# A mixture-of-experts stage with 33 static blocks of 64 rows and five weight slots

## The reference

```python
def hier_moe(xn, w_rg, b_rg, w_re, b_re, w_gate, w_up, w_down):
    t = xn.reshape(-1, D_MODEL)
    ...   # top-1 of 4 groups, then top-2 of its 8 experts: combine (576, 32), two entries a row
    def step(acc, xs):
        wg, wu, wd, c = xs                      # (1024, 256), (1024, 256), (256, 1024) float32
        hdn = jax.nn.silu(t @ wg) * (t @ wu)
        return acc + c[:, None] * (hdn @ wd).astype(jnp.float32), None
```

## Time and profile before

| | us |
|---|---|
| three runs of the kernel | 1416.87, 1423.91, 1422.7 |
| their median | 1422.7 |
| profiled execution: its own time as the page gives it, the span | 1420.8 |
| expert stage in it, first gate-and-up matmul to last copied result | 1003.6 to 1386.1 |
| after it, gather and final norm | 1386.1 to 1420.8 |

### The profile page before, as it was taken

How to read it: one execution, slowest core, us unless ns; L and a number is a source line. 1 busy time by engine, 2 the same in 40 slices (tenths; PEclk the granted TensorE clock), 3 DMA queues, 4 the chain that set the end, 5 groups by cost and what they waited for, 6 DMA issues and landing times.

```text
span 1420.8 us, 22301 instructions
## 1 busy us (share of the span) xinstructions
PE 1264.7 (89%) x8549; PEld 1130.7 (80%) x8549; DVE 796.2 (56%) x938; ACT 616.8 (43%) x819; POOL 67.5 (5%) x132
## 2 busy tenths in 40 slices
PE   5989999999999999999989989982788888888880
PEld 4989999999999999999989989982455555555550
DVE  4437374473755736547365444326567677677645
ACT  5434243343433434335343222232566666666632
POOL 0001010010100101001010000003000000000002
PEclk9999999999999999999999999965799999999995
DMA  5261121211121112121102235533888888888836
GB/s 186 95 208 54 58 71 61 72 47 61 65 67 56 61 61 65 53 71 61 63 22 80 80 103 164 211 136 127 293 319 322 321 323 325 316 329 328 313 126 220
DMA packets 49434, 212.80 MB, mean 150 GB/s; under 512 B 5920, under 2 KB 8496, under 8 KB 37104
## 3 DMA queue, kind: packets, MB, share of 16 engines
q1 hardware_dynamic: 41200, 194.05, 39.2%
q0 software_dynamic: 2928, 10.05, 2.1%
q10 hardware_dynamic: 5264, 8.13, 1.6%
HBM read 181.25 MB, written 30.96 MB: 149 GB/s over the span
## 4 chain that ended last, share of the span: by engine, by line
PE 78%; DVE 7%; ACT 6%; DMA 4%; issue 3%; POOL 1%; SPq 0%; ACTq 0%; DVEq 0%; POOLq 0%
PE proj L620 25%; PE proj L1337 15%; PE wideB L1358 6%; PE proj L987 5%; PE wideA L378 4%; PE proj L930 3%; PE wideB L370 3%; PE wideB L384 2%; PE wideA L1324 2%; DVE xbl L1426 2%; ACT xbh L1422 2%; PE small L987 2%; DMA wraw<-in_w_in 1%; PE small L1178 1%; POOL scr_rows L1783 1%
## 5 line engine op out<-in xcount | busy, mean ns | idle before, releaser
L620 PE MATMUL proj<-xnh,whi 128*128 128x288 f32 x1152 | 347.9, 302 | 11.1 <-DVE xnl L1868 6.3
L620 PE MATMUL proj<-xnl,whi 128*128 128x288 f32 x1152 | 347.2, 301 | 0.0
L620 PE MATMUL proj<-xnh,wlo 128*128 128x288 f32 x1152 | 347.0, 301 | 0.0
L620 PEld LDWEIGHTS proj<-xnh,whi 128*128 128x128 f32 x1152 | 217.9, 189 | 12.3 <-issue 5.7
L1414 DVE TENSOR_TENSOR elo<-eraw,ehi 128x4096 fp32r<-128x4096 f32 x64 | 214.6, 3354 | 19.8 <-ACT ehi L1404 19.8
L620 PEld LDWEIGHTS proj<-xnl,whi 128*128 128x128 f32 x1152 | 217.8, 189 | 0.0
L620 PEld LDWEIGHTS proj<-xnh,wlo 128*128 128x128 f32 x1152 | 217.8, 189 | 0.0
L1337 PE MATMUL proj<-ehi,xbh 128*80 128x512 f32 x256 | 111.0, 433 | 33.9 <-DVE xbl L1426 33.9
L632 DVE TENSOR_TENSOR wlo<-wraw,whi 128x1024 fp32r<-128x1024 f32 x72 | 95.1, 1321 | 58.1 <-ACT whi L628 57.1
L1404 ACT ACTIVATE ehi<-eraw 128x4096 fp32r<-128x4096 f32 x32 | 116.1, 3627 | 0.5
L1337 PE MATMUL proj<-elo,xbh 128*80 128x512 f32 x256 | 109.9, 429 | 0.0
(11 more groups left out here) (329 smaller groups left out, 2370.2 us busy)
## 6 DMA issues: line engine op xcount, KB each, us to landing
wraw<-in_w_in SPq DMA_DIRECT2D x72, 512.0 KB, 3.3
eraw<-in_w_gate SPq DMA_DIRECT2D x32, 1024.0 KB, 4.9
eraw<-in_w_up SPq DMA_DIRECT2D x32, 1024.0 KB, 7.2
eraw<-in_w_down SPq DMA_DIRECT2D x32, 1024.0 KB, 5.5
wraw<-in_w_out SPq DMA_DIRECT2D x24, 512.0 KB, 3.7
xb<-scr_rows SPq DMA_DIRECT2D x32, 320.0 KB, 6.0
scr_y<-yout SPq DMA_DIRECT2D x32, 320.0 KB, 5.7
scr_gate<-gate ACTq DMA_DIRECT2D x16, 288.0 KB, 2.1
```

The costliest lines, as they stand in the source:

```text
L620: mm = pe.matmul(out, w[:, kc, :], x[:, kc, hh * HALF:(hh + 1) * HALF], start=(j == 0), stop=(j == 23))
```

## The change

The expert stage is rebuilt; routing's arithmetic and phases 1, 2 and 5 stay.

- Blocks have 64 rows. 33 are static and written out without a loop: one for each expert, and one spare whose expert and place are read from routing's table. `further_blocks` runs what is left, with the same count less one.
- Rows are kept as one operand `xs` of 128 columns, 64 of the high part and 64 of the low. A gate-and-up product is two matmuls for each of eight chunks, high weights and low weights, whose 128 output rows hold the high rows' sums and the low rows'. ScalarE copies these (`sums_copied`), and four fp32 matmuls with a matrix `fold` add the two halves and transpose them at once. Low x low, not computed before, is now part of the sum.
- Silu, the product and the split of the hidden layer work on the turned hidden layer (128 partitions x 2 x 64).
- Weights have five slots. A slot holds gate/up (4096 columns) and down (2048); its low part is written in place over the loaded weights. `ehi` has two buffers, `dhi` (down, high) has one.
- SP fills slots 0 to 3 at the end of phase 2, slot 4 when the scatter is done, and then slot b % 5 as soon as block b-5 is through gate-and-up and down. Down weights are laid out in another order (4 KB pieces).
- GpSimd's queue takes over the load of each block's rows and the store of its result.
- In phase 3 only the gate/up weights of expert 0 are split; the down weights are split at the start of the expert stage.
- The inputs of the final sum are loaded three blocks ahead of the end.

The core of the diff:

```diff
-BR = 80
+BR = 64
+NB = EXPERTS + 1
+RING = 5
...
+    parts.append(i % BR == np.arange(BR)[None, :])
...
-        DOWN_AT = 12
+        DOWN_AT = 10
...
-            for j in range(3 * KC):
-                c, term = divmod(j, 3)
+            for j in range(2 * KC):
+                c, term = divmod(j, 2)
                 if between and j == DOWN_AT:
                     between()
-                x = (xbh, xbl, xbh)[term][k][:, c, :]
-                w = (ehi, ehi, elo)[term][k][:, 0:GU].rearrange("p (w c n) -> p w c n", w=2, c=KC)[:, :, c, :]
+                w = (ehi[k], elo[r])[term][:, :].rearrange("p (w c n) -> p w c n", w=2, c=KC)[:, :, c, :]
+                mm = pe.matmul(proj[k][:, :].rearrange("p (w n) -> p w n", w=2), xs[k][:, c, :], w, start=(j == 0),
+                               stop=(j == 2 * KC - 1))
...
+        def folded(pe, b):
+            pe.wait_ge(e_sum, b + 1)
+            wait(pe, e_hid, b)
+            for j in range(4):
+                mm = pe.matmul(proj[2][:, j * BR:(j + 1) * BR], ysum[b % 2][:, j * P:(j + 1) * P], fold,
+                               start=True, stop=True)
+            mm.then_inc(e_fold, 1)
...
         def phase4_tensor(pe):
+            rows_turned(pe, 0)
+            for b in range(NB):
+                gate_up(pe, b, b % RING, (lambda: down(pe, b - 1, (b - 1) % RING)) if b else None)
+                if b < NB - 1:
+                    rows_turned(pe, b + 1)
+                folded(pe, b)
+            down(pe, NB - 1, (NB - 1) % RING)
...
+        def weights_high(act, b, r):
+            act.wait_ge(e_w[r], 32 * (b // RING) + 32)
+            wait(act, e_gu, b - 1)
+            act.activation(ehi[b % 2][:, :], eraw[r][:, :], ACT.Copy).then_inc(e_high, 1)
+
+        def down_high(act, b, r):
+            act.wait_ge(e_wd[r], X_DONE + 16 * (b // RING) + 16)
+            wait(act, e_dn, b)
+            act.activation(dhi[:, :], draw[r][:, :], ACT.Copy).then_inc(d_high, 1)
+
+        def weights_low(dve, b, r):
+            dve.wait_ge(e_high, b + 1)
+            dve.tensor_tensor(elo[r][:, :], eraw[r][:, :], ehi[b % 2][:, :].bitcast(F32), ALU.subtract)\
+               .then_inc(e_low, 1)
+
+        def down_low(dve, b, r):
+            dve.wait_ge(d_high, b + 1)
+            dve.tensor_tensor(dlo[r][:, :], draw[r][:, :], dhi[:, :].bitcast(F32), ALU.subtract).then_inc(d_low, 1)
...
         def phase4_scalar(act):
+            down_high(act, 0, 0)
+            rows_high(act, 0, 0)
+            for b in range(NB):
+                if b < NB - 1:
+                    weights_high(act, b + 1, (b + 1) % RING)
+                if b:
+                    y_copy(act, b - 1, (b - 1) % 2)
+                    down_high(act, b, b % RING)
+                sums_copied(act, b, b % 2)
+                if b < NB - 1:
+                    rows_high(act, b + 1, (b + 1) % 2)
+                silu_gate(act, b)
+                hidden_high(act, b, b % 2)
+            y_copy(act, NB - 1, (NB - 1) % 2)
...
         def phase4_vector(dve):
+            down_low(dve, 0, 0)
             rows_low(dve, 0, 0)
+            for b in range(NB):
+                if b < NB - 1:
+                    weights_low(dve, b + 1, (b + 1) % RING)
+                if b:
+                    down_low(dve, b, b % RING)
+                if b < NB - 1:
+                    rows_low(dve, b + 1, (b + 1) % 2)
+                hidden_set(dve, b)
+                hidden_low(dve, b, b % 2)
...
+            for r in range(RING - 1):
+                gate_up_load(r, r, e_w[r])
+                down_load(r, r, e_wd[r])
...
             sp.wait_ge(spread_rows, 16 * 2 * UNITS)
+            gate_up_load(RING - 1, RING - 1, e_w[RING - 1])
+            down_load(RING - 1, RING - 1, e_wd[RING - 1])
+            for b in range(RING, NB):
+                r = b % RING
...
+                sp.wait_ge(e_gu, b - RING + 1)
+                gate_up_load(e, r, e_w[r])
+                sp.wait_ge(e_dn, b - RING + 1)
+                down_load(e, r, e_wd[r])
...
+            for b in range(2, NB):
+                if b == EXPERTS:
+                    pool.wait_ge(route, ROUTE_STEPS)
+                pool.wait_ge(e_xt, b - 1)
+                rows_load(b, b % 2)
+                if b > 2:
+                    y_store(b - 3, (b - 3) % 2)
```

## The result

The kernel after takes 1494.72 us (median of four runs, 1487.33 to 1499.93), the kernel before 1419.78 (four runs, 1414.04 to 1423.91): a ratio of 1.0512, 95% interval 1.0466 to 1.0558. It is slower, as forecast, but by 75 us where the forecast said about 25, and it lies outside the range.

A forecast was written before the change was run, and what follows sets the result against it. TensorE's order of work plus 1.6 us waiting for rows bound the expert stage. First block 9.0, 31 intervals 381.3, last block 16.5: 406.8 against 382.5, +24.3 on 1420.8, 1445.1; plus 1.9, so 1447 us, range 1419 to 1467.

The forecast's parts named there:

- I take 1.0 on loop two, 12.3: Expert stage: the low clock adds 1.0 us a block, between bounds 0 and 1.6, making each interval 12.3 us.
- loop two: Expert stage, through TensorE: `down_high`(b) waits on one `dhi` for down(b-1), then `down_low`, `rows_low`, next gate-and-up: 11.3 us at full clock.
- loop one: Expert stage, ScalarE and VectorE: weight splits, `down_low`, `rows_low`, `hidden_set`, `hidden_high` follow one another; sum 11.6, taken as 11.5 us.
- a whole dip: One low-clock stretch slowing TensorE's matmuls, priced at 1.6 us a block from the kernel before: 12.9 us an interval.
- TensorE's saving: Expert stage: gate and up go from 24 matmuls to 16; TensorE from about 9.6 to 8.2 us a block.
- nearly every block: Expert stage: a clock dip expected this often, since the gap without large matmuls grows from 2.6 to 4.5 us and more.
- Edits costed at nothing: Early fills, POOL-queue row loads and stores, earlier scatter, later first row load: taken as 0, the latter group bounded -1 and +2.
- Rival 1: Expert stage: the clock holds, ScalarE and VectorE pace at 11.5 us a block: -0.5, 1422 us; chance 0.13.
- Rival 2: Expert stage: a full 1.6 us clock dip in each block, 12.9 us: +43, 1466 us; chance 0.17.
- Rival 3: Expert stage: clock low for all 22 matmuls on the path through TensorE, 15.7 us a block: +130, 1552 us; chance 0.04.
- Rival 4: Expert stage: transfers at 337 GB/s are the true pace, 10.9 us a block: -19, 1403 us; chance 0.08.
- The signs named ahead: Expert stage: 4096-wide subtraction every 12 to 13 us, chain through `elo`, `dlo`, `dhi`, `yout`, rows; clock below 0.93; TensorE share falls.

The follow-up runs named there:

- the idle matmuls: Kernel after with ten 512-column matmuls more in each block, into a PSUM bank nothing reads, around the folds where the TensorE waits: 1419.87 us, ratio to before 0.9987.
- the fastest version: Kernel after with four slots, two `dhi` buffers, down splits a block ahead, six unread matmuls a block, ScalarE's down copy behind its rows copy: 1370.81 us, ratio to before 0.9676.

## Why the prediction was right in direction and too low

The sum, term by term, from the chain after: first block 8.8 (9.0 predicted), 31 intervals 421.0 (1011.64 to 1432.64; 381.3 predicted), last block 20.3 (16.5, whose terms as written add to 16.4). Together 43.3 too little, and 1447 + 43.3 is 1490.3, the profiled execution's time. Of the miss 39.7 lies in the intervals.

**The step that failed: "I take 1.0 on loop two, 12.3".** The clock's term measured 2.48 a block on loop two, 2.34 on the interval, since at the full clock loop one holds it at 11.31. The upper bound of 1.6, "a whole dip", was wrong too. The price of one slow matmul, 0.2, was right; the number of them was not: 2.48 is twelve of the 22, and 1.6 stands for eight. The 1.6 was taken from blocks of the kernel before, where the clock was low for 3.5 us; it was assumed that a dip keeps that length and that part of it falls in the gap, where it costs nothing. In the kernel after a low stretch lasts 6.8 us. 1.4 of it lie in the gap (from about 1199.1 to 1200.54), as assumed, but the other 5.4 cover all ten gate-and-up matmuls and the first of the down matmuls. The mechanism was right, the size was not: the price of a dip came from a loop with another gap, and was used as a bound. Why a low stretch lasts 6.8 us here and 3.5 before, no run separates. The last block's 3.8 are the same: 2.5 for its first 22 matmuls, 1.15 for the last twelve (5.35 for the 4.2 of "partly slow").

**Loop two** closes as written. From the end of the down matmuls at 1194.67 to the next start at 1200.54 are 5.87 us, priced 5.9; `y_copy` 1.02, `down_high` 1.90, `down_low` 2.29, `rows_low` 0.68 are within 0.01 of their prices, `rows_low` by size. With 5.31 for its matmuls at the full clock that is 11.2, 11.3 predicted. No run shows it by itself at that clock: in the second block of the kernel after (11.40) and with the idle matmuls (11.31) `down_low` starts right behind the 4096-wide subtraction, so these intervals are loop one's. **Loop one** is 11.3 in three experiments, 11.5 predicted.

**TensorE's saving** of 1.4 us a block went off the path. Its own work at full clock is 2.55 + 2.76 + 1.36 + 1.03 + 0.98 = 8.7 (8.2 predicted; transposes and folds were priced 0.2 and 0.1 too low, the matmuls 0.2), and the loop through the other engines is 11.3. The time saved became a longer gap in the TensorE's stream, and filling that gap took the clock's cost away.

**How often** a dip comes: "nearly every block" held: 30 of 31 intervals. By the Trainium skill, TensorE: Matmul & The Clock Gate, section HAM oscillation, a wait for a transfer that breaks the matmul stream in each tile makes every tile start at the lower clock. The trace of the kernel after agrees, and here the wait is for ScalarE and VectorE: from the third block on each block starts at 0.50. The price per block had to come from the trace, and the forecast took it from the wrong kernel.

**Edits costed at nothing.** Early fills: right (0.0 us of waiting, and two experiments). Row loads and stores on the POOL queue: right, none is in the chain between blocks. First row load "up to 1 us" later: 4.35. Scatter "up to 1 us" earlier: it took longer, 18.4 us from the first issue to the end of the last (970.37 to 988.79) for 16.8 before (976.38 to 993.21). The start of the stage moved by 0.8 in all, the stages ahead of it included, so none of this shows in the sum.

**The rivals.** Rival 1 (the clock holds and loop one paces, 1422) is what the kernel does when the clock is held for it: 1419.87. Rival 2 (a dip in each block) has the right mechanism at the wrong price, 12.9. Rival 3 (low throughout loop two, 15.7) goes too far: of the 22 matmuls the ten of gate-and-up and the first few of down were slow, then the clock rose. Rival 4 (transfers pace at 10.9) is refuted twice: 239 GB/s here, and 370 GB/s at intervals of 9.93 where the loops allow it. Its 337 GB/s was no ceiling by the forecast's own rows either: 389 GB/s stand in the line below it.

**The signs named ahead:** the 4096-wide subtraction recurs every 13.65, not 12 to 13; the clock (0.75) and TensorE's share of the stage (82% for 89%) fell; the chain does run through `yout` and `dhi`, and behind it through `dn_lo` and `xs`, but 57% of an interval (4.61 and 3.18 of 13.65) is still TensorE's matmuls, the first ten at half speed.

## What to carry to other kernels

When work is taken from a TensorE that waits for other engines once in each turn of a loop, write down every loop that runs through single buffers and through the order of the other engines' lists: here two of 11.2 and 11.3 us stood behind a TensorE need of 8.7, and one line moved on VectorE gave back all that the change had cost. Read the granted clock by stretches of the turn, not by its mean, and don't carry the price of a dip from one loop to another; a few matmuls into unused PSUM in the gap test in one run whether the clock is the cost (75 us here, 20 in the kernel before). Filling is a test first and a cure second: once the loops are shortened, the idle matmuls lie on the path themselves.

## What the runs showed of the hardware that was not expected

- The clock settled into a steady alternation with the loop: 6.7 us and more at 0.50, as long at 1.00, one of each to every interval of 13.65, from the third block to the last. It rises at about 1192.3, after 5.4 us of unbroken matmuls at 1.2 GHz, and falls at about 1199.1, after the transposes, 1.0 us of waiting and the folds. Every version with loop two uncut and no idle matmuls ends there: with 32 blocks the intervals go from 13.38 in the third block over 13.51 and 13.59 to 13.65 and stay. So the interval grows until it holds one low and one high stretch, and how many matmuls of a block fall into the low one is set by loop and alternation together.
- The first scatter issue on GpSimd took 5.29 us, the last 2.09, those between 0.9 to 1.3. Timelines of GpSimd and of VectorE, kernel after:

```profile
970.37 5.29 POOL L1826 DMA_INDIRECT scr_rows<-tn,slot_row  x1 [84.00 <-DVE block_table L1296]
986.70 2.09 POOL L1826 DMA_INDIRECT scr_rows<-tn,slot_row  x1 [0.30 <-issue]
...
970.32 4.42 DVE L1457 TENSOR_TENSOR gu_lo<-gu_raw,ehi 128x4096 fp32r<-128x4096 f32 x1
985.73 2.29 DVE L1462 TENSOR_TENSOR dn_lo<-dn_raw,dhi 128x2048 fp32r<-128x2048 f32 x1
```

  Both ran beside a subtraction of two SBUF operands, and ended 0.92 and 0.77 us after it. The Trainium skill, SBUF — State Buffer, section SBUF: two separate sides, says that a VectorE instruction with two SBUF inputs and a GpSimd one that reads SBUF exclude each other for the whole instruction; these rows agree. The kernel before agrees in two issues, the 3.96 of the earlier trace rows and the one behind it, and not in its first:

```profile
976.38 1.04 POOL L1783 DMA_INDIRECT scr_rows<-tn,slot_row  x1 [94.88 <-DVE block_table L1269]
...
976.34 6.70 DVE L1414 TENSOR_TENSOR elo<-eraw,ehi 128x4096 fp32r<-128x4096 f32 x2
```

  It began 0.05 after VectorE's, as the 5.29 one did, and was not held. No experiment took the subtraction away.
- A DMA share of 1.00 is no ceiling: 355 GB/s at 1.00 in the kernel after, 370 at 1.02 in the fastest version, 389 at 1.06 in the kernel before.
